# Two chunks per key-value step in alternating row halves, and the bf16 copy of the state moved to VectorE

## The chip, the cores and the metric

The kernel runs on all 8 cores of one Trainium2 chip. Each core computes one sequence of the batch of 8 on its own; there is no exchange between cores. The metric is the device time in microseconds of the slowest core. TensorE (PE in the profile) multiplies, ScalarE (ACT) applies functions, VectorE (DVE) does elementwise arithmetic, GpSimd (POOL) and SyncE (SP) only start transfers here.

## What is computed

Two layers over x of 8 x 4096 x 1024. The part that the change touches is the gated linear attention: per head (4 heads, keys of 128, values of 256) a state of 128 x 256 is carried from one chunk of 64 frames to the next, and every frame of a chunk reads the state at the end of its own chunk.

```python
proj = jnp.einsum('bsd,de->bse', h, w_in[l])
q, k, v, r, fz, gb_in, gc_in, cx, ga, gb = jnp.split(proj, split_pts, axis=-1)
...
kd = kc * jnp.exp(cum_end - cum)                  # decay of each key to chunk end (<= 1)
gamma = jnp.exp(cum_end[:, :, :, 0, :])           # whole-chunk decay (n_chunks,B,H,HEAD_K)
def step(state, inp):
    q_i, kd_i, v_i, g_i = inp
    state = g_i[..., None] * state + jnp.einsum('bhlk,bhlv->bhkv', kd_i, v_i)
    o_i = jnp.einsum('bhlk,bhkv->bhlv', q_i, state)
    return state, o_i
...
o = o * lax.rsqrt(jnp.mean(o * o, axis=-1, keepdims=True) + NORM_EPS) * gla_norm_g[l]
o = o.reshape(b_sz, s_len, VAL_WIDTH).astype(x.dtype) * jax.nn.silu(r)
y_a = jnp.einsum('bsv,vd->bsd', o, w_oa[l])
conv = causal_depthwise_conv(gc_in * cx, conv_w[l], conv_b[l])
y_b = jnp.einsum('bsc,cd->bsd', gb_in * conv, w_ob[l])
mix = jax.nn.sigmoid(ga) * y_a + jax.nn.sigmoid(gb) * y_b
x = x + jnp.einsum('bsd,de->bse', mix, w_o[l])
hid = jax.nn.silu(h2 @ w_ffn_gate[l]) * (h2 @ w_ffn_up[l])   # h2 = RMSNorm(x)
x = x + jnp.einsum('bsf,fd->bsd', hid, w_ffn_down[l])
```

## The kernel before, in words

A core works on tiles of 512 frames: 8 tiles per layer, 16 in all. A tile's token mixing (`mix_units`) and the feed-forward part of the tile before it (`ffn_units`) are lists of units with a cost; `woven` merges the two lists by these costs, and every engine gets its instructions in the order in which the units are then called. So the order on each engine is fixed when the program is built. Tile 0 has no feed-forward work beside it, the 15 tiles after it have.

A usual unit is a group of 8 matmuls of 128 x 512 (L278) into one of four PSUM banks, `banks`, which are handed round as a ring; the engine that reads the bank last gives it back. TensorE can thus run at most four units ahead of the engines that empty the banks. The units that matter here:

- `u_r` (8 per tile): the output gate r. ScalarE computes the sigmoid in three steps, L300, L302, L304, and VectorE multiplies (L307, output in `dgm`) and frees the bank. `u_g` of the feed-forward part is of the same kind (output in `sg`), `u_u` needs only VectorE (L307, output in `hid`).
- `u_C`, `u_X`, `u_B` (8 each per tile): the convolution branch, with L519 on ScalarE and L307, L537, L540, L542 on VectorE.
- `g_U` (8 calls per tile, 128 in all): the key-value products. A slice `ts` of 128 frames holds two chunks, c = 0 in partitions 0 to 63 and c = 1 in partitions 64 to 127. Each call issues four matmuls with 64 rows, then VectorE updates four states (L454) and ScalarE copies each to bf16 (L458).
- `g_C` (4 calls per tile): eight matmuls of queries with the bf16 states (L472), then on ScalarE four squares with sums (L482), L486 and L488, then L492 on VectorE. `g_T`: transposes (L504), copied by VectorE (L511).

In the list, `g_U` stands behind unit ts*8 and behind unit ts*8+2 of the r and convolution units, `g_C` behind ts*8+5, `g_T` behind ts*8+9. The eight r units come first, so the two calls of `g_U` and the `g_C` of slice 0 lie among them.

`Eng.after` sets a wait only if the engine hasn't yet waited for that value. The banks of `g_U` are `BU = (4, 5)`, which the norms use too (`BN1`, `BN2`). S32 are four states in fp32, S16 are eight bf16 copies, one for each chunk and head.

Of the kernel before, what the change touches and what calls it, by code (L numbers as in the profile page):

```python
# [8 lines left out]
AF = mybir.ActivationFunctionType  # L9
ALU = mybir.AluOpType  # L10
# [79 lines left out]
def build_nc(S):  # L90
# [12 lines left out]
    with ExitStack() as es:  # L103
        newsem = lambda n: es.enter_context(nc.semaphore(n))
        sb = lambda n, s, d: es.enter_context(nc.sbuf_tensor("sb_" + n, s, d))
        pe = Eng(nc.tensor, newsem("s_pe"))
        act = Eng(nc.scalar, newsem("s_act"))
        dve = Eng(nc.vector, newsem("s_dve"))
        pool = Eng(nc.gpsimd, newsem("s_pool"))
        sp = Eng(nc.sync, newsem("s_sp"))  # L110
        V, A, P = nc.vector, nc.scalar, nc.tensor
# [6 lines left out]
        kd = sb("kd", [128, NTS, 512], BF16)  # L118
# [214 lines left out]
        def mix_units(i):  # L333
# [2 lines left out]
            us = []  # L336
            loc = {"spb": [None] * 4, "dec": [None] * 4, "v": [None] * 8, "kd": [None] * 4, "q": [None] * 4,
                   "grs": [[None, None] for _ in range(4)], "og": [None] * 4, "ogT": [None] * 4, "gbc": [None] * 8,
                   "mix": [None] * 8, "sg": {}, "S16": {}, "x": [None] * 8, "sp_used": None, "nmm": None, "n2mm": None}

            def add(cost, blk, fn):
                us.append(Unit(cost, (i, BIDX[blk]) if blk else None, fn))
# [92 lines left out]
                sg.give(buf, loc["grs"][ts][hf])  # L435


            def g_U(ts, c):
                pr = slice(c * 64, (c + 1) * 64)
                for hp in range(2):  # L440
                    pe.after(loc["kd"][ts], loc["v"][hp * 4 + ts], st["U_free"][hp])
                    for h2_ in range(2):
                        hh = hp * 2 + h2_
                        ins = P.matmul(pb[BU[hp]][:, h2_ * 256:(h2_ + 1) * 256], kd[pr, ts, hh * 128:(hh + 1) * 128],  # L444
                                       vog[pr, ts, hh * 256:(hh + 1) * 256], start=True, stop=True)
                    k = pe.do(ins)
# [408 lines left out]
```

How the kernel before makes its waits and increments, by code:

```python
    def after(self, *toks):  # L57
        for tk in toks:
            if tk is None:
                continue
            sem, val = tk
            if self.seen.get(id(sem), 0) < val:
                self.h.wait_ge(sem, val)
                self.seen[id(sem)] = val
# [1 line left out]
    def do(self, ins):  # L66
        ins.then_inc(self.sem, 1)
        self.n += 1
        return (self.sem, self.n)
# [20 lines left out]
def build_nc(S):  # L90
# [74 lines left out]
        def load(q, dst, src, name):
            s = newsem(name)
            q.h.dma_start(out=dst, in_=src).then_inc(s, 16)
            return (s, 16)
        t_id = load(act, ident32[:], cst_d[:, 0:128], "c_id")
        t_msk = load(act, msk[:], cst_d[:, 128:258], "c_msk")
        t_pk = load(act, pk[:], pk_d, "c_pk")
        wfg_sem = newsem("c_wfg")
        nc.scalar.dma_start(out=wfg[0:17, :], in_=wfg_d[0]).then_inc(wfg_sem, 16)
        t_wfg = (wfg_sem, 16)
        t_ones = dve.do(V.memset(ones16[:], 1.0 / D))
        t_eps = dve.do(V.memset(epsb[:], EPS))
# [20 lines left out]
        def load_x(i):  # L199
            l, t = divmod(i, NT)
            b = i % 3
            if xs_n[b]:
                sp.after((xstore[b], xs_n[b]))
            if l == 0:
                src = x_d[:, t * T:(t + 1) * T].rearrange("(c p) s -> p c s", p=128)
            else:
                sp.after(spill[t])
                src = xs_d[t].rearrange("p (c s) -> p c s", c=KC)
            nc.sync.dma_start(out=xT[b][:], in_=src).then_inc(xland[b], 16)
            xl_n[b] += 16
            st["x", i] = (xland[b], xl_n[b])
```

## Time and profile before

| | |
|---|---|
| median of 3 runs | 5062.94 us |
| profiled execution, time | 5063.73 us |
| its span (core 7, the slowest) | 5062.7 us |
| spans of the 8 cores | 5041.4 to 5062.7 us |
| mean granted TensorE clock, core 7 | 0.975 |
| busy share: PE, ACT, DVE, POOL | 95%, 44%, 41%, 4% |

TensorE is busy almost all the time; the other engines matter where it waits for them. The views used are the waits of each engine (who waited for whom, and how long), the timeline (instructions in order of time, those of a kind merged), the groups of instructions, and the windows (busy time of each engine in a stretch).

### The profile page before, as it was taken

To read this page: it belongs to the slowest core of one execution; us is meant where nothing else is said; L and a number is where in the kernel's file an instruction comes from. 1 tells how busy PE (TensorE), PEld (TensorE's weight loads), DVE (VectorE), ACT (ScalarE), POOL (GpSimd) and SP (SyncE) were. 2 spreads that over 40 slices of the span, in tenths; PEclk is the share of its full clock that TensorE was granted. 3 is DMA by queue.
4 is the path that set the end of the run, shared out by engine and by line. 5 is a ranking of instruction groups with operands and counts; after the bars stand their busy time and mean duration, and the time that the engine had idled before them with its cause. 6 is when DMAs were issued, how large, how long until landed. Compare 5 with 4: busy or idle time off the path is not lost.

```text
span 5062.7 us, 66511 instructions; the slowest of 8 cores (5041.4 to 5062.7 us)
## 1 busy us (share of the span) xinstructions
PE 4811.1 (95%) x22464; PEld 2165.7 (43%) x22464; DVE 2086.6 (41%) x3486; ACT 2218.1 (44%) x4481; POOL 189.8 (4%) x362
## 2 busy tenths in 40 slices
PE   6999999999999999999899999999999999999998
PEld 2444444444444444444344444434444444444443
DVE  2544353433535345253252534435344353443633
ACT  3454353544535444353343544435344354543533
POOL 0000000000000000000000000000000000000000
PEclk9999999999999999999899999999999999999999
DMA  6768989786553444444567888877755444343343
GB/s 136 136 130 153 193 158 207 180 201 185 168 183 127 138 158 142 154 140 139 126 134 172 146 163 176 174 190 181 190 192 165 159 140 148 140 150 137 134 153 116
DMA packets 131197, 798.91 MB, mean 158 GB/s; under 512 B 13074, under 2 KB 13330, under 8 KB 66612
## 3 DMA queue, kind: packets, MB, share of 16 engines
q0 software_dynamic: 51552, 336.81, 34.3%
q1 hardware_dynamic: 78866, 457.64, 26.2%
q8 instruction: 189, 3.10, 0.2%
q14 instruction: 140, 1.15, 0.1%
q10 hardware_dynamic: 450, 0.22, 0.0%
HBM read 936.24 MB, written 114.36 MB: 208 GB/s over the span
## 4 chain that ended last, share of the span: by engine, by line
PE 81%; ACT 6%; DMA 4%; DVE 4%; issue 3%; ACTq 0%; DVEq 0%; POOL 0%; SPq 0%; POOLq 0%
PE pb L278 75%; ACT sb_sg L302 2%; ACT sb_sg L300 2%; DMA scr<-sb_wsl 2%; DVE sb_h L329 1%; PE pb L404 1%; DMA sb_wsl<-w 1%; PE pb L317 1%; PE pb L444 1%; PE pb L393 1%; ACT sb_sg L304 1%; DVE sb_xT L329 1%; DMA sb_xT<-x 1%; PE pb L380 1%; ACT sb_sqj L482 1%
## 5 line engine op out<-in xcount | busy, mean ns | idle before, releaser
L278 PE MATMUL pb<-sb_h,sb_wsl 128*128 128x512 bf16 (+1 forms) x11392 | 2630.3, 384 | 86.5 <-DVE sb_dgm L307 32.5
L278 PEld LDWEIGHTS pb<-sb_h,sb_wsl 128*128 128x128 bf16 (+1 forms) x11392 | 1103.8, 99 | 1478.7 <-issue 242.7
L307 DVE TENSOR_TENSOR sb_sg<-pb,sb_sg 128x512 f32<-128x512 f32 x608 | 418.2, 691 | 1485.2 <-ACT sb_sg L304 1012.3
L300 ACT ACTIVATE sb_sg<-pb 128x512 f32<-128x512 f32 x736 | 434.4, 590 | 1178.5 <-PE pb L278 1178.3
L278 PE MATMUL pb<-sb_hid,sb_wsl 128*128 128x512 bf16 x2816 | 631.4, 380 | 9.7 <-DMA sb_wsl<-w 7.5
L278 PE MATMUL pb<-sb_wsl,sb_h 128*128 128x512 bf16 x2560 | 621.2, 392 | 5.3 <-DVE sb_sg L307 3.5
L302 ACT ACTIVATE sb_sg<-sb_sg 128x512 f32<-128x512 f32 x736 | 464.1, 631 | 69.8 <-ACT sb_sg L300 3.0
L304 ACT ACTIVATE sb_sg<-sb_sg 128x512 f32<-128x512 f32 x736 | 464.0, 630 | 68.8 <-ACT sb_sg L302 1.8
L278 PEld LDWEIGHTS pb<-sb_hid,sb_wsl 128*128 128x128 bf16 x2816 | 275.4, 98 | 344.3 <-issue 19.1
L278 PEld LDWEIGHTS pb<-sb_wsl,sb_h 128*128 128x128 bf16 x2560 | 253.5, 101 | 355.4 <-issue 93.3
L313 ACT ACTIVATE sb_sq<-sb_xT 128x512 bf16<-128x512 f32 x320 | 195.9, 623 | 403.7 <-DVE sb_xT L604 322.3
L307 DVE TENSOR_TENSOR sb_hid<-pb,sb_sg 128x512 bf16<-128x512 f32 x352 | 241.7, 687 | 212.6 <-PE pb L278 206.5
L715 DVE TENSOR_TENSOR sb_xT<-pb,sb_xT 128x512 f32<-128x512 f32 x128 | 88.4, 691 | 584.2 <-PE pb L278 584.2
L458 ACT ACTIVATE sb_S<-sb_S 128x256 bf16<-128x256 f32 x512 | 203.2, 417 | 261.5 <-DVE sb_S L454 260.2
L278 PE MATMUL pb<-sb_vog,sb_wsl 128*128 128x512 bf16 x1024 | 255.4, 395 | 33.5 <-DVE sb_vog L511 33.5
L238 POOL DMA_DIRECT2D sb_wsl<-w x272 | 143.9, 530 | 3671.4 <-PE pb L278 2853.8
L278 PE MATMUL pb<-sb_dgm,sb_wsl 128*128 128x512 bf16 x1024 | 241.7, 379 | 16.3 <-DVE sb_dgm L583 16.3
L278 PE MATMUL pb<-sb_sgc,sb_wsl 128*128 128x512 bf16 x1024 | 243.0, 380 | 0.0
L454 DVE SCALAR_TENSOR_TENSOR sb_S<-sb_S,sb_gam,pb 128x256 f32<-128x256 f32 x512 | 210.7, 473 | 0.0
L329 DVE SCALAR_TENSOR_TENSOR sb_h<-sb_xT,sb_pk,sb_rstd 128x512 bf16<-128x512 f32 x256 | 180.6, 744 | 59.7 <-ACT sb_rstd L326 59.7
L317 PE MATMUL pb<-sb_sq,sb_ones 128*128 128x512 bf16 x320 | 115.7, 384 | 60.2 <-ACT sb_sq L313 60.2
L278 PEld LDWEIGHTS pb<-sb_vog,sb_wsl 128*128 128x128 bf16 x1024 | 101.6, 100 | 162.3 <-issue 50.5
(58 smaller groups left out, 2404.5 us busy)
## 6 DMA issues: line engine op xcount, KB each, us to landing
sb_wsl<-scr SPq DMA_DIRECT2D x248, 1024.0 KB, 5.1
sb_wsl<-w POOLq DMA_DIRECT2D x168, 1024.0 KB, 10.4
sb_wsl<-scr SPq DMA_DIRECT2D x76, 768.0 KB, 4.9
sb_wsl<-scr SPq DMA_DIRECT2D x80, 704.0 KB, 4.2
scr<-sb_wsl POOLq DMA_DIRECT2D x52, 1024.0 KB, 13.6
sb_wsl<-w POOLq DMA_DIRECT2D x52, 768.0 KB, 8.4
sb_wsl<-w POOLq DMA_DIRECT2D x48, 704.0 KB, 8.7
sb_xT<-x SPq DMA_DIRECT2D x8, 2048.0 KB, 20.8
```

The source lines that it names most:

```text
L238: nc.gpsimd.dma_start(out=wsl[s][:, 0:n], in_=blk_ap(w_d, l, bi)).then_inc(wsem_p[s], 16)
L278: ins = P.matmul(out, a, b, start=(j == 0), stop=(j == n - 1))
L300: k = act.do(A.activation(out=buf[:], in_=pb[b][:, :], func=AF.Exp, scale=-1.0))
L302: k = act.do(A.activation(out=buf[:], in_=buf[:], func=AF.Ln, bias=1.0))
L304: return buf, act.do(A.activation(out=buf[:], in_=buf[:], func=AF.Exp, scale=-1.0))
L307: return V.tensor_tensor(out=out, in0=a, in1=b, op=ALU.mult)
L313: k = act.do(A.activation(out=buf[:], in_=xT[xb][:, dc, :], func=AF.Square))
L317: kk = pe.do(P.matmul(pb[bank][:, :], ones16[:, :], buf[:], start=(dc == 0), stop=(dc == KC - 1)))
L329: return V.scalar_tensor_tensor(out=out, in0=xT[xb][:, dc, :], scalar=pkc(gcol), in1=rs[:], op0=ALU.mult, op1=ALU.mult)
L454: ks = dve.do(V.scalar_tensor_tensor(out=S32[hh][:], in0=S32[hh][:], scalar=gam[:, g:g + 1], in1=pb[BU[hp]][:, h2_ * 256:(h2_ + 1) * 256], ...
L458: loc["S16"][hh] = act.do(A.activation(out=S16[si][:], in_=S32[hh][:], func=AF.Copy))
L715: k = dve.do(V.tensor_tensor(out=xT[xb][:, dc, :], in0=pb[b][:, :], in1=xT[xb][:, dc, :], op=ALU.add))
```

## The change: what it does

A call of `g_U` no longer takes one chunk and four heads, but two heads and both chunks. Its four matmuls alternate between rows 0 to 63 and rows 64 to 127, and chunk c writes bank `BU[c]` where before head pair hp wrote `BU[hp]`. One wait for both banks stands ahead of all four. VectorE then updates the two states for chunk 0, copies them to bf16 itself, updates them for chunk 1 and copies them. ScalarE's 512 copies are gone. Numbers and sizes of all other instructions stay.

```diff
-            def g_U(ts, c):
-                pr = slice(c * 64, (c + 1) * 64)
-                for hp in range(2):
-                    pe.after(loc["kd"][ts], loc["v"][hp * 4 + ts], st["U_free"][hp])
-                    for h2_ in range(2):
-                        hh = hp * 2 + h2_
-                        ins = P.matmul(pb[BU[hp]][:, h2_ * 256:(h2_ + 1) * 256], kd[pr, ts, hh * 128:(hh + 1) * 128],
+            def g_U(ts, hp):
+                pe.after(loc["kd"][ts], loc["v"][hp * 4 + ts], st["U_free"][0], st["U_free"][1])
+                for h2_ in range(2):
+                    hh = hp * 2 + h2_
+                    for c in range(2):
+                        pr = slice(c * 64, (c + 1) * 64)
+                        ins = P.matmul(pb[BU[c]][:, h2_ * 256:(h2_ + 1) * 256], kd[pr, ts, hh * 128:(hh + 1) * 128],
                                        vog[pr, ts, hh * 256:(hh + 1) * 256], start=True, stop=True)
...
+                for c in range(2):
                     for h2_ in range(2):
                         hh = hp * 2 + h2_
                         g = ts * 8 + hh * 2 + c
-                        si = (c * 4 + hh)
-                        dve.after(k, loc["gam"], st["S32"][hh], loc["S16"].get(hh))
+                        dve.after(k, loc["gam"], st["S32"][hh])
                         ks = dve.do(V.scalar_tensor_tensor(out=S32[hh][:], in0=S32[hh][:], scalar=gam[:, g:g + 1],
-                                                           in1=pb[BU[hp]][:, h2_ * 256:(h2_ + 1) * 256], op0=ALU.mult, op1=ALU.add))
+                                                           in1=pb[BU[c]][:, h2_ * 256:(h2_ + 1) * 256], op0=ALU.mult, op1=ALU.add))
                         st["S32"][hh] = ks
-                        act.after(ks, st["S16_used"][si])
-                        loc["S16"][hh] = act.do(A.activation(out=S16[si][:], in_=S32[hh][:], func=AF.Copy))
-                        loc["S16", c, hh] = loc["S16"][hh]
-                        st["gam_used"] = ks
-                    st["U_free"][hp] = ks
+                    st["U_free"][c] = ks
+                    for h2_ in range(2):
+                        hh = hp * 2 + h2_
+                        si = c * 4 + hh
+                        dve.after(st["S32"][hh], st["S16_used"][si])
+                        loc["S16", c, hh] = dve.do(V.tensor_copy(out=S16[si][:], in_=S32[hh][:]))
+                st["gam_used"] = ks
```

On TensorE, the second call of slice 0 in the sixth tile (kd holds the keys, vog the values, pb4 and pb5 are the two banks), before:

```order
L278 MATMUL pb3<-sb_h2,sb_wsl0 128x512 x7
L444 MATMUL pb4<-sb_vog,sb_kd 128x256 [waits s_dve]
L444 MATMUL pb4<-sb_vog,sb_kd 128x256
L444 MATMUL pb5<-sb_vog,sb_kd 128x256 [waits s_dve]
L444 MATMUL pb5<-sb_vog,sb_kd 128x256
L278 MATMUL pb0<-sb_wsl3,sb_h1 128x512 [waits s_dve]
```

The same place now:

```order
L278 MATMUL pb3<-sb_h2,sb_wsl0 128x512 x7
L445 MATMUL pb4<-sb_vog,sb_kd 128x256 [waits s_dve]
L445 MATMUL pb5<-sb_vog,sb_kd 128x256
L445 MATMUL pb4<-sb_vog,sb_kd 128x256
L445 MATMUL pb5<-sb_vog,sb_kd 128x256
L278 MATMUL pb0<-sb_wsl3,sb_h1 128x512 [waits s_dve]
```

Still four key-value matmuls between the same two units, but neighbours now use different row halves and different banks, and the second wait has moved to the front.

On VectorE, the same call, before (sb_S32 are the states, sb_dgm the output of an r unit):

```order
L307 TENSOR_TENSOR sb_sg0<-pb3,sb_sg0 128x512 [waits s_act]
L454 SCALAR_TENSOR_TENSOR sb_S32_0<-sb_S32_0,sb_gam,pb4 128x256 [waits s_pe,s_dve]
L454 SCALAR_TENSOR_TENSOR sb_S32_1<-sb_S32_1,sb_gam,pb4 128x256 [waits s_dve]
L454 SCALAR_TENSOR_TENSOR sb_S32_2<-sb_S32_2,sb_gam,pb5 128x256 [waits s_pe,s_dve]
L454 SCALAR_TENSOR_TENSOR sb_S32_3<-sb_S32_3,sb_gam,pb5 128x256 [waits s_dve]
L307 TENSOR_TENSOR sb_dgm<-pb0,sb_sg1 128x512 [waits s_act]
```

And now:

```order
L307 TENSOR_TENSOR sb_sg0<-pb3,sb_sg0 128x512 [waits s_act]
L455 SCALAR_TENSOR_TENSOR sb_S32_2<-sb_S32_2,sb_gam,pb4 128x256 [waits s_pe]
L455 SCALAR_TENSOR_TENSOR sb_S32_3<-sb_S32_3,sb_gam,pb4 128x256
L463 CAST sb_S16_2<-sb_S32_2 128x256 [waits s_dve]
L463 CAST sb_S16_3<-sb_S32_3 128x256 [waits s_dve]
L455 SCALAR_TENSOR_TENSOR sb_S32_2<-sb_S32_2,sb_gam,pb5 128x256
L455 SCALAR_TENSOR_TENSOR sb_S32_3<-sb_S32_3,sb_gam,pb5 128x256
L463 CAST sb_S16_6<-sb_S32_2 128x256 [waits s_dve]
L463 CAST sb_S16_7<-sb_S32_3 128x256 [waits s_dve]
L307 TENSOR_TENSOR sb_dgm<-pb0,sb_sg1 128x512 [waits s_act]
```

Between the same two neighbours VectorE has eight instructions where it had four.

On ScalarE, the same call, before:

```order
L304 ACTIVATE sb_sg0<-sb_sg0 128x512 [waits s_act]
L458 ACTIVATE sb_S16_4<-sb_S32_0 128x256 [waits s_dve]
L458 ACTIVATE sb_S16_5<-sb_S32_1 128x256 [waits s_dve]
L458 ACTIVATE sb_S16_6<-sb_S32_2 128x256 [waits s_dve]
L458 ACTIVATE sb_S16_7<-sb_S32_3 128x256 [waits s_dve]
L300 ACTIVATE sb_sg1<-pb0 128x512 [waits s_pe]
```

And now:

```order
L302 ACTIVATE sb_sg0<-sb_sg0 128x512 [waits s_act]
L304 ACTIVATE sb_sg0<-sb_sg0 128x512 [waits s_act]
L300 ACTIVATE sb_sg1<-pb0 128x512 [waits s_pe,s_dve]
L302 ACTIVATE sb_sg1<-sb_sg1 128x512 [waits s_act]
L304 ACTIVATE sb_sg1<-sb_sg1 128x512 [waits s_act]
```

The next sigmoid (L300 on bank 0) follows the one before it directly; the four copies, with their waits for VectorE, no longer stand between.

## Rows read from the trace of the kernel before

**Rows 1.** The page's first line.

```profile
span 5062.7 us, 66511 instructions; the slowest of 8 cores (5041.4 to 5062.7 us)
```

**Rows 2.** TensorE's waits: us in total, times, longest us.

```profile
PE pb L278 <- DVE sb_dgm L307: 34.0, 28, 1.9
...
PE pb L278 <- DMA sb_wsl<-w: 14.1, 4, 5.8
...
PE pb L278 <- DVE sb_hid L307: 7.5, 8, 2.2
```

**Rows 3.** Groups by line: busy us, mean ns | idle before, releaser.

```profile
L444 PE MATMUL pb<-sb_vog,sb_kd 64*128 64x256 bf16 x512 | 78.3, 272 | 3.7 <-DVE sb_S L454 3.7
...
L458 ACT ACTIVATE sb_S<-sb_S 128x256 bf16<-128x256 f32 x512 | 203.2, 417 | 261.5 <-DVE sb_S L454 260.2 <-issue 1.3
```

**Rows 4.** Timeline, one call of g_U: start us, us, engine, line.

```profile
1300.79 0.38 PE L278 MATMUL pb<-sb_h,sb_wsl 128*128 128x512 bf16 x1
1301.10 0.61 PE L444 MATMUL pb<-sb_vog,sb_kd 64*128 64x256 bf16 x4
...
1301.64 0.39 PE L278 MATMUL pb<-sb_h,sb_wsl 128*128 128x512 bf16 x1
```

**Rows 5.** Timeline, one call of g_C.

```profile
1316.34 0.38 PE L278 MATMUL pb<-sb_h,sb_wsl 128*128 128x512 bf16 x1
...
1316.65 0.63 PE L472 MATMUL pb<-sb_S,sb_qT 128*64 128x256 bf16 x8
...
1317.21 0.39 PE L278 MATMUL pb<-sb_h,sb_wsl 128*128 128x512 bf16 x1
```

**Rows 6.** Timeline of the sixth tile, around the second call for slice 0.

```profile
1561.12 1.89 PE L278 MATMUL pb<-sb_wsl,sb_h 128*128 128x512 bf16 x8
...
1564.08 0.69 DVE L307 TENSOR_TENSOR sb_sg<-pb,sb_sg 128x512 f32<-128x512 f32 x1 [1.24 <-ACT sb_sg L304]
...
1564.57 3.62 PE L278 MATMUL pb<-sb_wsl,sb_h 128*128 128x512 bf16 x16
1564.68 1.64 DVE L454 SCALAR_TENSOR_TENSOR sb_S<-sb_S,sb_gam,pb 128x256 f32<-128x256 f32 x4
1565.25 1.59 ACT L458 ACTIVATE sb_S<-sb_S 128x256 bf16<-128x256 f32 x4 [1.27 <-DVE sb_S L454]
1566.74 0.58 ACT L300 ACTIVATE sb_sg<-pb 128x512 f32<-128x512 f32 x1
...
1569.15 0.69 DVE L307 TENSOR_TENSOR sb_dgm<-pb,sb_sg 128x512 bf16<-128x512 f32 x1 [2.82 <-ACT sb_sg L304]
...
1569.99 1.89 PE L278 MATMUL pb<-sb_h,sb_wsl 128*128 128x512 bf16 x8 [1.80 <-DVE sb_dgm L307]
```

**Rows 7.** The same tile, 10 us later, behind g_C of slice 0.

```profile
1577.49 0.58 ACT L300 ACTIVATE sb_sg<-pb 128x512 f32<-128x512 f32 x1
1577.56 1.89 PE L278 MATMUL pb<-sb_h,sb_wsl 128*128 128x512 bf16 x8
...
1580.46 1.89 PE L278 MATMUL pb<-sb_h,sb_wsl 128*128 128x512 bf16 x8 [1.01 <-DVE sb_dgm L307]
```

**Rows 8.** VectorE groups, SBUF to SBUF with one tensor operand.

```profile
L537 DVE TENSOR_SCALAR sb_csb<-sb_ub,sb_pk 128x512 f32<-128x512 f32 x128 | 69.9, 546 | 14.2 <-DVE sb_ub L307 0.5
...
L181 DVE CAST sb_ident<-sb_ident 128x128 bf16<-128x128 f32 x1 | 0.2, 227 | 1.4 <-DMA sb_ident<-cst 1.4
```

**Rows 9.** Timeline of the sixth tile, second call for slice 2.

```profile
1617.39 8.81 PE L278 MATMUL pb<-sb_h,sb_wsl 128*128 128x512 bf16 x40
...
1621.01 1.65 DVE L454 SCALAR_TENSOR_TENSOR sb_S<-sb_S,sb_gam,pb 128x256 f32<-128x256 f32 x4
1622.58 0.68 DVE L307 TENSOR_TENSOR sb_sgc<-pb,sb_csb 128x512 bf16<-128x512 f32 x1
```

**Rows 10.** Window in tile 0: PE, PEld, DVE, ACT, POOL busy us (xcount), clock, DMA.

```profile
115.00:175.00 60.00, 53.04 (x283) 23.81 (x281) 47.40 (x91) 31.29 (x99) 4.22 (x8) 1.00 0.74 130
```

**Rows 11.** GpSimd's weight loads, from the page's groups.

```profile
L238 POOL DMA_DIRECT2D sb_wsl<-w x272 | 143.9, 530 | 3671.4 <-PE pb L278 2853.8
```

More of the change, by code:

```diff
@@ L338, in mix_units @@
                    "grs": [[None, None] for _ in range(4)], "og": [None] * 4, "ogT": [None] * 4, "gbc": [None] * 8,
-                   "mix": [None] * 8, "sg": {}, "S16": {}, "x": [None] * 8, "sp_used": None, "nmm": None, "n2mm": None}
+                   "mix": [None] * 8, "sg": {}, "x": [None] * 8, "sp_used": None, "nmm": None, "n2mm": None}
             def add(cost, blk, fn):
@@ L435, in u_r @@
                 sg.give(buf, loc["grs"][ts][hf])
-            def g_U(ts, c):
-                pr = slice(c * 64, (c + 1) * 64)
-                for hp in range(2):
-                    pe.after(loc["kd"][ts], loc["v"][hp * 4 + ts], st["U_free"][hp])
-                    for h2_ in range(2):
-                        hh = hp * 2 + h2_
-                        ins = P.matmul(pb[BU[hp]][:, h2_ * 256:(h2_ + 1) * 256], kd[pr, ts, hh * 128:(hh + 1) * 128],
+            def g_U(ts, hp):
[5 more added lines that the diff above has]
+                        ins = P.matmul(pb[BU[c]][:, h2_ * 256:(h2_ + 1) * 256], kd[pr, ts, hh * 128:(hh + 1) * 128],
                                        vog[pr, ts, hh * 256:(hh + 1) * 256], start=True, stop=True)
-                    k = pe.do(ins)
-                    loc["U", ts] = k
-                    st["kd_used"] = k
+                k = pe.do(ins)
+                loc["U", ts] = k
+                st["kd_used"] = k
+                for c in range(2):
                     for h2_ in range(2):
```

## The prediction

> **What bounds the kernel now.** I read the page first: TensorE is busy 95% of a span of 5062.7 us [rows 1], ScalarE 44% and VectorE 41%. So a faster ScalarE or VectorE is worth nothing by itself. Two things count: time that TensorE's own work takes, and the places where TensorE waits. For these the view is TensorE's waits [rows 2]: the largest entry that the other engines' attention work can touch is that for `dgm`, the output of the r units, 34.0 us in 28 waits; beside it stand 7.5 us for `hid`, which VectorE issues right behind it, and 14.1 us for weight loads, which the edit does not touch. Then comes the timeline around such a wait in an ordinary tile [rows 6, 7], since a wait for VectorE need not be VectorE's fault. The profiled execution took 5063.73 us, 0.8 us over the median of 5062.94, so a sum made against the trace holds for the median too.
>
> **Part 1, the four products in alternating row halves.** Before, a call's four matmuls of 256 columns use the same 64 rows. They start 0.113 us apart, (0.61 - 0.27) / 3 [rows 3, 4], so each streams alone. From the last ordinary matmul ahead (1300.79) to the first behind (1301.64) pass 0.85 us; less one ordinary pitch of 0.22 us (1.73 us for a unit of eight, which is 8.81 less the last one's 0.38, over 39 [rows 9]) the call costs 0.63 us. The trace does not show row halves side by side, so I bound the gain. One end is nothing: the halves take turns, and the call stays at 0.63. The other is the nearest row, `g_C` [rows 5], which uses half the array in columns: its eight matmuls of the same 256 columns cost 1317.21 - 1316.34 - 0.22 = 0.65 us, as much as four of `g_U`. So there two share the time of one. If alternating rows do the same, two pitches of 0.113 go from each call, less some nanoseconds: 0.20 us. Over 128 calls that is 25.5 us, all of it on TensorE, which is the bound. I take this end, since `g_C` is the same engine with the same column count and the new order puts independent halves and separate banks next to each other. A loss is excluded by the count: no matmul, weight load or switch between full and half array is added, each call had one of either before.
>
> **Part 2, ScalarE loses 512 copies** (203.2 us of busy time, and another 261.5 us in which it stood in front of them waiting, nearly all of it for L454 [rows 3]). Most of this ran beside other work. Where it does not is seen in rows 6. TensorE runs the r unit of bank 0 from 1561.12, done by 1563.01. ScalarE would be free for its sigmoid right behind the sigmoid that VectorE reads at 1564.08, that is at about 1564.0, but next in its queue are the four copies, and these wait for the updates, which VectorE starts only at 1564.68. So the sigmoid starts at 1566.74, 2.7 us late; VectorE multiplies at 1569.15, and TensorE, four banks ahead, waits for bank 0 and resumes at 1569.99. Its last matmul had started at 1564.57 + 3.62 - 0.38 = 1567.81, so it could have gone on at 1568.03: 1.96 us lost, of which the profile calls 1.80 a wait.
>
> With the copies gone from ScalarE the product is ready for VectorE at about 1569.15 - 2.74 = 1566.4. Now VectorE is next late: its group is longer by four casts. Their duration is not in the trace at this size. The nearest rows are the cast of 128 elements, 227 ns, and the one-tensor operation of 512, 546 ns [rows 8]; between them 256 elements come to 333 ns. Ends: 227 ns, and 546 ns. Queued instructions overlap by 0.08 us (L454 takes 0.47 and has a pitch of (1.64 - 0.47) / 3 = 0.39), so I take a pitch of 0.25 us, 1.0 us for four. The group before took 1622.58 - 1621.01 = 1.57 us to the next instruction [rows 9]. Then L307 starts at 1564.68 + 1.57 + 1.0 = 1567.25, TensorE 0.84 us later (as 1569.15 to 1569.99) at 1568.09, against 1568.03 if nothing held it. The stall is gone but for 0.06 us. I count 1.8 us for each of the 15 tiles that have feed-forward work beside them: 27 us. That the sixth tile is typical follows from the sums: (34.0 + 7.5) / 15 = 2.8 us of waits per tile [rows 2], and it has 1.80 + 1.01 [rows 6, 7].
>
> The second stall of the tile [rows 7] stands behind `g_C`, whose squares and sums keep ScalarE's queue. TensorE's last matmul there started at 1577.56 + 1.89 - 0.38 = 1579.07, and it resumes at 1580.46: 1.17 us lost. ScalarE is 2.74 us earlier at the first place and TensorE 1.96, so at most 0.8 of the 1.17 can go, and nothing need go if ScalarE then waits for its own inputs. I take 0.5: 15 x 0.5 = 7.5 us. Together part 2 gives 34.5 us.
>
> **Part 3, what the longer group on VectorE costs.** Queued behind it are the multiplications that free TensorE's banks. The tightest place that I found outside the r units is in rows 9: L307 ends at 1623.26 and frees the bank that the unit starting at 1617.39 + 4 x 1.73 = 1624.31 needs, 1.05 us to spare, of which 0.15 is the release itself (1569.99 less 1569.84). So 0.9 us covers an addition of 1.0: 0.1 x 15 = 1.5 us lost. In tile 0, without feed-forward units between, VectorE is busy 47.4 of 60 us [rows 10] and TensorE waits for it already; six calls fall there, 6 x 1.0 = 6 us if all is exposed, nothing if ScalarE's relief covers it. I take 4. The wait for both banks at the front of a call costs nothing in the other tiles: the updates that free bank 5 end at 1622.66, and the next call is behind the 40 matmuls. `g_C` now waits for VectorE's casts in place of ScalarE's copies: it stood 3 units behind them and keeps that. If this cover fails each cast costs its 0.25 us.
>
> **Sum:** 5063.7 - 25.5 - 34.5 + 1.5 + 4 = 5009.2, so 5009 us, 1.1% below.
>
> **Rivals.**
>
> 1. The halves take turns (or the products are done one by one for another reason; the change then does not do what it says on TensorE). For it: no row shows row halves overlapping, and in `g_C` neighbours in the order are of the same column half, so what overlaps there is not fully clear. Time: 5009 + 25.5 = 5035.
> 2. The ScalarE stall is replaced by one of VectorE of the same size: VectorE is behind for a reason of its own, and the wait at `dgm` keeps its length. For it: after the change VectorE is the one that is late at rows 6, by my own sum only 0.06 us from the point. Against: the earlier copies also held ScalarE back, so the whole stretch should run earlier. Time: 5009 + 34.5 = 5044.
> 3. Slower: casts that do not overlap, since each follows an update that it depends on. With 546 ns each and 0.1 us between, the group grows by a = 2.6 us. The first stall keeps a - 0.94 = 1.66 of its 1.96 us (gain 0.3 x 15 = 4.5), the place in rows 9 loses a - 0.9 = 1.7 x 15 = 25.5, tile 0 loses 6 x 2.6 = 15.6: 5063.7 - 25.5 - 4.5 + 25.5 + 15.6 = 5075. It decides from a of about 2.3 us (gains 25.5 + 9, losses 21 + 13.8). Against it: the 227 ns of the cast in rows 8.
> 4. More is gained: both stalls go whole (1.96 + 1.17 = 3.1 us, 15 x 3.0 = 45) and tile 0 costs nothing: 5063.7 - 25.5 - 45 = 4993.
> 5. The casts delay GpSimd's weight loads. There are 272 [rows 11]; TensorE waits for them 14.1 us in four waits [rows 2]. If a load lands later by a call's four casts, 4 x 0.33 = 1.3 us, and a quarter of them have no time to spare, 68 x 1.3 = 88 us: 5097. It turns the result from (5063.7 - 5009) / 1.3 = 42 such loads. The Trainium skill states such a rule (SBUF — State Buffer, Who interferes with whom): a VectorE copy or cast from SBUF to SBUF may take the port pair that it shares with GpSimd, and GpSimd, which writes the descriptors of its own DMAs, is then shut out for the whole instruction. The trace speaks neither for nor against: VectorE's one-tensor operations of 546 ns [rows 8] are already there beside these loads, and the loads' only long waits are for TensorE to free a slot [rows 11], which suggests time to spare.
>
> **How the numbers follow.** The forecast, 5009 with some 10 us either way for the terms that I split, has 0.55; rival 4 has 0.12, rival 1 0.12, rival 2 0.10, rival 3 0.06, rival 5 0.02, and 0.03 is left for what I have not seen. The range goes from 4988 (rival 4 and 5 us for a TensorE clock that changes level at other moments) to 5044 (rival 2, which with rival 1 it takes in); rivals 3 and 5 are left out. A measurement of this kernel can tell a change from none at about 2%, 101 us. All stalls and the products together are worth 71 us, so faster by more than that has 0.01; slower by more needs rival 5 at twice its price, 0.01; within it 0.98.
>
> **What would show it.** A call on TensorE of 0.43 us, its four starts in two pairs; if they stay 0.11 apart, part 1 is wrong. No wait for `dgm` of over 1 us in the r stretch; if one stays, the timeline must tell whether VectorE's casts or a sigmoid came last. Casts of 0.33 us with a pitch of 0.25. VectorE busy some 128 to 170 us more, ScalarE 203 us less. In tile 0 some microseconds more of waits for the updates. I would be wrong altogether if VectorE's group ran past 3.9 us, or if waits for weight loads grew beyond their 14.1 us.

## The result, and the profile after

The changed kernel took 4998.45, 5006.16 and 5009.74 us, the kernel before 5062.35 and 5062.94 in the same comparison; the ratio is 0.9886, with a 95% interval of 0.9857 to 0.9914. That is 1.1% or 57.7 us less: clear of no change by its interval, but under the 2% that the prediction named as the bound. One execution of the change (5521.09) and two of before (5207.78, 5729.62) had a die at a lower clock and are left out, which is why the medians over all executions, 5007.95 against 5135.36, lie 2.5% apart. The profiled execution after is that of 4998.45 us.

The page of the kernel after, its first lines:

```profile
span 4997.4 us, 65713 instructions; the slowest of 8 cores (4979.2 to 4997.4 us)
...
PE 4736.9 (95%) x22021; PEld 2137.6 (43%) x22464; DVE 2185.6 (44%) x3998; ACT 2025.8 (41%) x3969; POOL 190.5 (4%) x362
```

The same line of the page before:

```profile
PE 4811.1 (95%) x22464; PEld 2165.7 (43%) x22464; DVE 2086.6 (41%) x3486; ACT 2218.1 (44%) x4481; POOL 189.8 (4%) x362
```

The span fell from 5062.7 us [rows 1] by 65.3 us. VectorE was busy 2086.6 us before and 2185.6 now, ScalarE 2218.1 and 2025.8. TensorE's busy sum has 443 matmul records fewer than the 22464 weight loads, so it can't be set against that of before; starts and waits can.

TensorE's waits after (us in total, times, longest us):

```profile
PE pb L278 <- DVE sb_vog L514: 33.3, 15, 3.8
...
PE pb L278 <- DMA sb_wsl<-w: 15.2, 5, 4.8
...
PE pb L445 <- DVE sb_S L455: 6.7, 4, 2.1
PE pb L278 <- DVE sb_dgm L307: 5.8, 8, 1.0
PE pb L278 <- DVE sb_hid L307: 4.6, 8, 2.2
PE pb L475 <- DVE sb_S L463: 1.1, 2, 0.7
```

Against [rows 2] the wait for `dgm` went from 34.0 to 5.8 us and that for `hid` from 7.5 to 4.6, together 31.1 us. Waits for weight loads stand at 15.2 against 14.1. Waits for the states grew: the products' for the updates from 3.7 us [rows 3] to 6.7, and `g_C` now waits 1.1 us for the casts. All of these stand in tile 0.

The groups of after that answer to [rows 3] and [rows 11]:

```profile
L445 PE MATMUL pb<-sb_vog,sb_kd 64*128 64x256 bf16 x512 | 50.2, 274 | 6.7 <-DVE sb_S L455 6.7
...
L463 DVE CAST sb_S<-sb_S 128x256 bf16<-128x256 f32 x512 | 125.1, 284 | 1.4 <-DVE sb_S L463 1.3
...
L238 POOL DMA_DIRECT2D sb_wsl<-w x272 | 144.3, 531 | 3612.5 <-PE pb L278 2687.5
```

One matmul of the products lasts as long as before, 274 against 272 ns, but the 512 together cover 50.2 us of the clock on the wall against 78.3: they overlap. The new casts take 284 ns, and VectorE stood idle only 1.4 us ahead of all of them.

The timeline of one call of `g_U` after, against [rows 4]:

```profile
1538.26 0.38 PE L278 MATMUL pb<-sb_wsl,sb_h 128*128 128x512 bf16 x1
1538.57 0.39 PE L445 MATMUL pb<-sb_vog,sb_kd 64*128 64x256 bf16 x4
1538.89 0.39 PE L278 MATMUL pb<-sb_wsl,sb_h 128*128 128x512 bf16 x1
```

Four products now last 0.39 us where they lasted 0.61. In the records of single matmuls the starts stand at 0, 3, 119 and 123 ns, in two pairs, where before they stood at 0, 120, 229 and 338. From the last ordinary matmul to the next ordinary one pass 0.636 us, the median of the calls, against 0.852.

The timeline of after at the place of [rows 6], the second call for slice 0 in the sixth tile:

```profile
1548.28 0.60 ACT L300 ACTIVATE sb_sg<-pb 128x512 f32<-128x512 f32 x1
1548.47 0.69 DVE L307 TENSOR_TENSOR sb_sg<-pb,sb_sg 128x512 f32<-128x512 f32 x1 [1.24 <-ACT sb_sg L304]
...
1549.08 0.86 DVE L455 SCALAR_TENSOR_TENSOR sb_S<-sb_S,sb_gam,pb 128x256 f32<-128x256 f32 x2
...
1549.69 3.62 PE L278 MATMUL pb<-sb_wsl,sb_h 128*128 128x512 bf16 x16
...
1549.86 0.49 DVE L463 CAST sb_S<-sb_S 128x256 bf16<-128x256 f32 x2
1550.26 0.86 DVE L455 SCALAR_TENSOR_TENSOR sb_S<-sb_S,sb_gam,pb 128x256 f32<-128x256 f32 x2
1551.04 0.48 DVE L463 CAST sb_S<-sb_S 128x256 bf16<-128x256 f32 x2
1551.45 0.68 DVE L307 TENSOR_TENSOR sb_dgm<-pb,sb_sg 128x512 bf16<-128x512 f32 x1
...
1553.14 1.89 PE L278 MATMUL pb<-sb_h,sb_wsl 128*128 128x512 bf16 x8
```

The sigmoid of bank 0 starts at 1548.28, ahead of the updates, where before it stood behind the copies. VectorE multiplies for `dgm` right behind its last cast, and is done at 1552.13; TensorE's last matmul starts at 1549.69 + 3.62 - 0.38 = 1552.93 and the next r unit follows it at 1553.14 with no wait, 1.0 us after the product was ready. And at the place of [rows 7], behind `g_C`:

```profile
1560.60 0.60 ACT L300 ACTIVATE sb_sg<-pb 128x512 f32<-128x512 f32 x1 [0.22 <-issue]
1560.72 1.89 PE L278 MATMUL pb<-sb_h,sb_wsl 128*128 128x512 bf16 x8
...
1562.74 0.69 DVE L307 TENSOR_TENSOR sb_dgm<-pb,sb_sg 128x512 bf16<-128x512 f32 x1 [0.53 <-ACT sb_sg L304]
...
1563.58 1.89 PE L278 MATMUL pb<-sb_h,sb_wsl 128*128 128x512 bf16 x8 [0.97 <-DVE sb_dgm L307]
```

This one is still there, 0.97 us against 1.01, for ScalarE still comes out of `g_C`'s squares late. On this core the sixth tile lost more at it (1.13 us) than the other tiles of the layer (0.85). All the waits for `dgm` that are left are of this kind.

**The account.** Products: 128 calls x (0.852 - 0.636) = 27.6 us. Waits for `dgm` and `hid`: 31.1 us. Another way to count the second gives nearly the same on every core: in the stretch of the r units of the 15 tiles, the sum of what TensorE's starts came late beyond their pitch of 0.217 us fell from 43.1 to 10.6 us. Together 58.7 us. Against it, the waits for the states in tile 0 grew by 4.1 us, while the transposes' wait there for `ogtok`, 1.5 us before, is gone:

```profile
PE pb L504 <- DVE sb_ogtok L492: 1.5, 1, 1.5
```

That leaves 56.1 us, beside the 57.7 of the ratio. The mean of the eight spans, 5051.9 before, is 4987.9, 4991.6 and 4994.1 in the three executions after: 57.8 to 64.0 us less. So the account closes within the spread of the executions.

### The profile page after: what moved, and what is told of

Its sections match the earlier page's. It is cut to its first block, busy times and chain, and to the rows that moved or that the text cites. A ratio compares the mean times of both kernels' runs of the same rounds, so it can differ in the third digit from the quotient of the medians.

```text
span 4997.4 us, 65713 instructions; the slowest of 8 cores (4979.2 to 4997.4 us)
## 1 busy us (share of the span) xinstructions
PE 4736.9 (95%) x22021; PEld 2137.6 (43%) x22464; DVE 2185.6 (44%) x3998; ACT 2025.8 (41%) x3969; POOL 190.5 (4%) x362
## 3 DMA queue, kind: packets, MB, share of 16 engines
q1 hardware_dynamic: 78866, 457.64, 26.2%
## 4 chain that ended last, share of the span: by engine, by line
PE 82%; DMA 7%; DVE 5%; ACT 4%; issue 3%; POOL 0%; DVEq 0%; ACTq 0%; POOLq 0%; SPq 0%
PE pb L278 76%; DMA scr<-sb_wsl 3%; DMA sb_wsl<-w 2%; DVE sb_h L329 1%; PE pb L404 1%; PE pb L317 1%; PE pb L393 1%; ACT sb_sg L302 1%; ACT sb_sg L300 1%; DVE sb_xT L329 1%; DMA sb_xT<-x 1%; ACT sb_sg L304 1%; PE pb L445 1%; PE pb L475 1%; DVE sb_sg L307 1%
## 5 line engine op out<-in xcount | busy, mean ns | idle before, releaser
L278 PE MATMUL pb<-sb_h,sb_wsl 128*128 128x512 bf16 (+1 forms) x11139 | 2608.4, 384 | 80.5 <-DVE sb_fza L365 26.7
L278 PEld LDWEIGHTS pb<-sb_h,sb_wsl 128*128 128x128 bf16 (+1 forms) x11392 | 1103.0, 99 | 1451.1 <-issue 211.3
L307 DVE TENSOR_TENSOR sb_sg<-pb,sb_sg 128x512 f32<-128x512 f32 x608 | 418.0, 691 | 1403.0 <-ACT sb_sg L304 935.7
L300 ACT ACTIVATE sb_sg<-pb 128x512 f32<-128x512 f32 x736 | 435.4, 592 | 1286.7 <-PE pb L278 1229.9
L278 PE MATMUL pb<-sb_hid,sb_wsl 128*128 128x512 bf16 x2774 | 631.2, 381 | 13.4 <-DMA sb_wsl<-w 7.9
L278 PE MATMUL pb<-sb_wsl,sb_h 128*128 128x512 bf16 x2494 | 604.5, 387 | 10.8 <-DVE sb_sg L307 4.5
L278 PEld LDWEIGHTS pb<-sb_hid,sb_wsl 128*128 128x128 bf16 x2816 | 276.2, 98 | 346.9 <-issue 22.8
L278 PEld LDWEIGHTS pb<-sb_wsl,sb_h 128*128 128x128 bf16 x2560 | 251.6, 100 | 346.9 <-issue 80.7
L307 DVE TENSOR_TENSOR sb_hid<-pb,sb_sg 128x512 bf16<-128x512 f32 x352 | 241.7, 687 | 204.6 <-PE pb L278 198.5
L278 PE MATMUL pb<-sb_vog,sb_wsl 128*128 128x512 bf16 x1024 | 255.4, 395 | 33.4 <-DVE sb_vog L514 33.3
L278 PE MATMUL pb<-sb_dgm,sb_wsl 128*128 128x512 bf16 x987 | 239.6, 379 | 18.2 <-DVE sb_dgm L586 16.3
L278 PE MATMUL pb<-sb_sgc,sb_wsl 128*128 128x512 bf16 x979 | 235.1, 379 | 2.4
L455 DVE SCALAR_TENSOR_TENSOR sb_S<-sb_S,sb_gam,pb 128x256 f32<-128x256 f32 x512 | 221.1, 473 | 0.0
L536 ACT ACTIVATE sb_halo<-sb_ub 128x2 f32<-128x2 f32 x128 | 26.0, 204 | 359.6 <-DVE sb_ub L307 359.6
L278 PEld LDWEIGHTS pb<-sb_vog,sb_wsl 128*128 128x128 bf16 x1024 | 101.8, 100 | 163.2 <-issue 52.3
## 6 DMA issues: line engine op xcount, KB each, us to landing
sb_wsl<-w POOLq DMA_DIRECT2D x168, 1024.0 KB, 10.9
```

The lines of the kernel that those rows point to most:

```text
L278: ins = P.matmul(out, a, b, start=(j == 0), stop=(j == n - 1))
L300: k = act.do(A.activation(out=buf[:], in_=pb[b][:, :], func=AF.Exp, scale=-1.0))
L307: return V.tensor_tensor(out=out, in0=a, in1=b, op=ALU.mult)
```

## The experiments

In each diff + and - are against the changed kernel, except for the second, whose is against the kernel before. Below, "late starts" is the sum just told: 43.1 us before, 10.6 us after.

**One: the pairs alone, copies on ScalarE.** This undoes part 2. The updates write one state per head, so each must wait for the copy of the one before.

```diff
-                        dve.after(k, loc["gam"], st["S32"][hh])
+                        dve.after(k, loc["gam"], st["S32"][hh], st.get(("cp", hh)))
...
-                        dve.after(st["S32"][hh], st["S16_used"][si])
-                        loc["S16", c, hh] = dve.do(V.tensor_copy(out=S16[si][:], in_=S32[hh][:]))
+                        act.after(st["S32"][hh], st["S16_used"][si])
+                        loc["S16", c, hh] = act.do(A.activation(out=S16[si][:], in_=S32[hh][:], func=AF.Copy))
+                        st["cp", hh] = loc["S16", c, hh]
```

> Part 1 alone: the four products alternate between the row halves as in the change, but ScalarE makes the bf16 copies. Since chunk 1 overwrites the same fp32 state in the same call, VectorE must now wait in the middle of its group for ScalarE's copies of chunk 0. Theory (the two parts are independent gains, the products are worth 27.6 us = 128 x 0.216 us): about 5035 us against 5063 before, and the wait for dgm stays at some 34 us. Rival (the two parts need each other: the middle wait holds up both queues): waits for dgm grow to 50 us or more and the time comes out at 5045 to 5065, most of the products' gain given back.

It took 5056.79 and 5064.24 us, against 5058.12 to 5064.35 for the kernel before on the same chip (and once 5092.06): nothing gained that the slowest core shows; no interval is on record for it. Yet the call takes 0.636 us as in the change. TensorE's waits of this kernel:

```profile
PE pb L278 <- DVE sb_dgm L307: 49.4, 31, 3.3
...
PE pb L278 <- DVE sb_hid L307: 5.3, 5, 2.2
```

The timeline of it at the second call for slice 0 of a tile:

```profile
1571.76 0.86 DVE L455 SCALAR_TENSOR_TENSOR sb_S<-sb_S,sb_gam,pb 128x256 f32<-128x256 f32 x2
...
1572.32 0.81 ACT L463 ACTIVATE sb_S<-sb_S 128x256 bf16<-128x256 f32 x2 [1.27 <-DVE sb_S L455]
...
1572.84 0.87 DVE L455 SCALAR_TENSOR_TENSOR sb_S<-sb_S,sb_gam,pb 128x256 f32<-128x256 f32 x2 [0.22 <-ACT sb_S L463]
...
1573.42 0.81 ACT L463 ACTIVATE sb_S<-sb_S 128x256 bf16<-128x256 f32 x2 [0.29 <-DVE sb_S L455]
1574.13 0.58 ACT L300 ACTIVATE sb_sg<-pb 128x512 f32<-128x512 f32 x1
```

Now both engines wait for each other in the middle of the group: chunk 1's updates for chunk 0's copies (0.22), then ScalarE for these updates (0.29). The sigmoid starts 2.37 us after the first update, where in [rows 6] it was 1566.74 - 1564.68 = 2.06. Late starts grew to 57 to 61 us on the eight cores, some 16 us more than before, which takes back more than half of the 27.6. They are not waits alone: behind the longest of them TensorE's matmuls start 0.43 us apart for a while and not 0.22, at a granted clock of 0.55 in such a stretch (core 7, 963 to 966 us), and 2 to 6 us of each core's sum are of this kind. The mean of the eight spans is 5042.1 and 5048.1 us, against 5047.1 to 5055.2 before on that chip (5058.6 in the long one), so some 6 us are left of the gain. The rival held, with 49.4 us of waits where it said 50 or more: the products in pairs need the copies moved. With one state per head, the order that pairs them also ties the copies between the updates.

**Two: the casts alone, products in the old order.**

```diff
-                        dve.after(k, loc["gam"], st["S32"][hh], loc["S16"].get(hh))
+                        dve.after(k, loc["gam"], st["S32"][hh])
...
-                        act.after(ks, st["S16_used"][si])
-                        loc["S16"][hh] = act.do(A.activation(out=S16[si][:], in_=S32[hh][:], func=AF.Copy))
...
+                    for h2_ in range(2):
+                        hh = hp * 2 + h2_
+                        si = c * 4 + hh
+                        dve.after(st["S32"][hh], st["S16_used"][si])
+                        loc["S16", c, hh] = dve.do(V.tensor_copy(out=S16[si][:], in_=S32[hh][:]))
```

> Part 2 alone: a call takes one chunk and four heads as before, its products one after another in one row half, but VectorE makes the bf16 copies. Theory: a call on TensorE still costs 0.63 us, the first stall of a tile (1.96 us) goes, the second shrinks by 0.3 to 0.7 us: 5063 - 15 x 2.3 = 5029 us, waits for dgm under 8 us. Rival (the stalls went because the shorter calls gave VectorE and ScalarE time): waits for dgm stay near 34 us and the time near 5063.

Measured: ratio 0.9938 (0.9905 to 0.9971), 5023.89, 5029.92, 5033.28 and 5052.54 us; the profiled execution is the last. Its waits:

```profile
PE pb L278 <- DVE sb_dgm L307: 5.8, 8, 1.0
PE pb L278 <- DVE sb_hid L307: 4.6, 8, 2.2
```

They are those of the change to the tenth, late starts are 10.6 us, and the call still takes 0.852 us. So part 2 alone removes the stalls, and does nothing else.

**Three: another order within the call.** First both heads of chunk 0, then both of chunk 1, so that neighbours in the order use the same 64 rows.

```diff
-                for h2_ in range(2):
-                    hh = hp * 2 + h2_
-                    for c in range(2):
+                for c in range(2):
+                    for h2_ in range(2):
+                        hh = hp * 2 + h2_
```

> The change with its four products in another order: both heads of chunk 0 (rows 0 to 63), then both of chunk 1. Same banks, same waits, same work elsewhere. Theory (two products share time only if they are neighbours in different row halves): only the second and third overlap, a call costs 0.11 us more than in the change, 128 x 0.11 = 14 us: about 5022 us, starts at 0, 0.12, 0.12 and 0.23 us. Rival (any two products of a call in half-array tiles overlap, as the neighbours of the same column half seem to do in g_C): the same as the change, 5008 us.

Measured: ratio 0.988 (0.9842 to 0.9918), 5003.62 to 5012.05 us. The timeline of a call:

```profile
1564.90 0.38 PE L278 MATMUL pb<-sb_h,sb_wsl 128*128 128x512 bf16 x1
1565.21 0.40 PE L445 MATMUL pb<-sb_vog,sb_kd 64*128 64x256 bf16 x4
1565.54 0.39 PE L278 MATMUL pb<-sb_h,sb_wsl 128*128 128x512 bf16 x1
```

The call takes 0.640 us, the same as with neighbours in alternate halves, and the records show the starts at 0, 7, 119 and 126 ns. My theory that each must find its partner right beside it would have lost half of the gain, and it fell. What counts is that both row halves have work within the call. The records don't name the half of a product, so which two start together is not shown. The doubt in rival 1 has the same answer: in `g_C` [rows 5], where two products of one column half stand before two of the other, the eight starts come in pairs too, 7 ns apart.

**Four: longer casts.** Each of the casts issued twice, the second waiting for the first.

```diff
-                        loc["S16", c, hh] = dve.do(V.tensor_copy(out=S16[si][:], in_=S32[hh][:]))
+                        for _ in range(2):
+                            loc["S16", c, hh] = dve.do(V.tensor_copy(out=S16[si][:], in_=S32[hh][:]))
+                            dve.after(loc["S16", c, hh])
```

> The change with every bf16 cast on VectorE issued twice, each waiting for the one before: a call's group on VectorE grows by four casts, some 1.6 us at 0.28 us and 0.1 us between, from 2.37 to about 4.0 us. It measures the cover of VectorE. Theory (VectorE's queue has about 1.0 us to spare at the first stall and 0.3 us at the place of the second call of slice 2): 0.6 us comes back per tile at the first and 1.3 us at the other, and tile 0 loses 6 x 1.6 us: 15 x 1.9 + 10 = 38 us, about 5046 us. Rival (VectorE is idle over half of the time and covers it): within 8 us of the change.

None of its times (5452.9 us and up) can be set against the others. But single cores can: the 18 whose granted clock was 0.967 or more took 5101.5 to 5157.7 us, 5136 in the mean, where such cores of the kernel before took 5060 on that chip. With the 57.7 us that the change gains, this is some 130 us above the change, over three times what I had expected. Part of it is that the dose was larger: VectorE's group took 4.80 us in the median, not 4.0, since casts that wait for each other start 0.40 us apart. The waits of its core 7:

```profile
PE pb L278 <- DVE sb_sgc L307: 54.2, 39, 2.8
PE pb L278 <- DVE sb_hid L307: 24.4, 31, 2.2
PE pb L278 <- DVE sb_dgm L307: 18.0, 31, 1.1
```

The largest new wait is not in the r stretch but behind slice 2 (`sgc`), the place of [rows 9]. For a price from whole executions I tried a smaller dose.

**Five: two casts more per call.** Chunk 1's two are issued again.

```diff
+                    for h2_ in range(2 * c):
+                        hh = hp * 2 + h2_
+                        si = c * 4 + hh
+                        dve.after(loc["S16", c, hh])
+                        loc["S16", c, hh] = dve.do(V.tensor_copy(out=S16[si][:], in_=S32[hh][:]))
```

> The changed kernel with the two casts of chunk 1 issued a second time: a call's group on VectorE grows by two casts, some 0.5 to 0.6 us. It measures VectorE's cover with half the dose of the run with every cast doubled. Theory (the tightest place outside the r units has 0.1 to 0.3 us to spare, the first stall 1.0 us): 0.4 us lost per tile outside the r stretch, 0.2 in it, 3 us in tile 0: about 12 us over the change, ratio 0.991. Rival (cover is exceeded at several places of a tile at once): 25 us or more, ratio above 0.993, with waits for sgc and hid that the change does not have.

Measured: ratio 0.9913 (0.9896 to 0.993), where the change itself, run beside it, has 0.9888; 0.25%, 12.7 us, about what I had expected, though the intervals overlap. The group grew by 0.40 us (2.78 against 2.37). But the loss is not where I had put it. Of its waits:

```profile
PE pb L278 <- DVE sb_dgm L307: 5.8, 8, 1.0
...
PE pb L278 <- DVE sb_sgc L307: 3.2, 8, 0.7
```

The wait for `dgm` did not move, and late starts in the r stretch are 10.9 us; a stretch later, at `sgc`, TensorE is late by 4 to 5.4 us in all, where the change has 0 to 1.3. So the tight place is that of [rows 9], and the r stretch has cover. The other 8 us are in no wait, and most of them are in the clock: 384 ordinary matmuls of a core, in the mean, start 0.43 us after the one before them and not 0.22, against 337 in the change beside it. At 0.21 us each that is 9.8 us, though such counts differ by 18 between two executions of the change (319 and 337).

**Six: copies on ScalarE again, but with a state of their own for chunk 0,** so that chunk 1's updates need not wait for a copy. Eight states in place of four, the first plan, don't fit: 416 bytes of a partition's SBUF are left where the squares' scrap output needs 512, so that version has no result. This one has six, and to make room, the scrap output of the squares shares memory with the 32-bit identity matrix, which has been read by then.

```diff
-        S32 = [sb("S32_%d" % h, [128, 256], F32) for h in range(4)]
+        S32 = [sb("S32_%d" % h, [128, 256], F32) for h in range(6)]
...
-                        ks = dve.do(V.scalar_tensor_tensor(out=S32[hh][:], in0=S32[hh][:], scalar=gam[:, g:g + 1],
+                        ks = dve.do(V.scalar_tensor_tensor(out=(S32[hh] if c else S32[4 + h2_])[:], in0=(S32[4 + h2_] if c else S32[hh])[:], scalar=gam[:, g:g + 1],
```

> Products in pairs, copies on ScalarE, and two more fp32 states in place of four: chunk 0 of a call writes a state of its own, from which ScalarE copies and chunk 1 updates, so VectorE waits in a call for no copy of that call. (The scrap output of L482 shares memory with a constant that is no longer read.) Against the first run (one set of states, 49.4 us of waits for dgm) it gives the price of the middle wait. Theory (that wait is what costs): waits for dgm back to about 34 us, time 5035 us or ratio 0.994. Rival (ScalarE's copies cost as much wherever VectorE waits, because they come in two halves of a call now): waits stay near 49 us, ratio 0.999.

Measured: ratio 0.9962 (0.9946 to 0.9977), 5048.77 to 5053.47 us. Its waits:

```profile
PE pb L278 <- DVE sb_dgm L307: 41.9, 33, 2.3
...
PE pb L278 <- DVE sb_hid L307: 7.4, 8, 2.2
```

Late starts are 50.5 us. So the wait in the middle of the group, seen in experiment one, costs about 8 us (57 to 61 less 50.5, the lower clock behind it included), and copies that come in two halves on ScalarE cost some 7 us beyond those of before (50.5 less 43.1). My theory had only the first: waits for `dgm` are 41.9 us, halfway between its 34 and the rival's 49. The sum closes: 27.6 - 7.4 = 20.2 us, and 0.38% of 5063 is 19.2.

**Seven and eight: the largest wait that is left.** The biggest entry that this part of the kernel has after the change is `L278 <- DVE sb_vog`, 33.3 us: the gate units that follow `u_v` wait for VectorE's copies of `vog`. The edit puts the transposes of slice 3, `g_T(3)`, ahead of the first two gate units.

```diff
-                add(8, n, lambda dc=dc: u_gate(dc, 0))
-                add(8, n, lambda dc=dc: u_gate(dc, 1))
                 if dc == 0:
                     add(3, None, lambda: g_T(3))
+                add(8, n, lambda dc=dc: u_gate(dc, 0))
+                add(8, n, lambda dc=dc: u_gate(dc, 1))
```

> The change with the last g_T of a tile put ahead of the first two gate units in place of behind them. It is a trial for a faster version: in the changed kernel TensorE waits 33.3 us in 15 waits for VectorE's copy of that transpose, and runs 8 matmuls at the lower clock behind each such wait of 3.7 us. Theory: with two units between the transpose and its first reader the wait goes whole, and the clock stays up: 15 x (2.2 + 1.7) = 58 us, about 4950 us. Rival (VectorE's copy is queued behind a product that waits for ScalarE, and stays late): 10 to 25 us, 4985 to 4998 us.

> The early transpose again, beside the change on one chip. Theory: the change's 33.3 us of waits for vog are gone, about 2.2 us in each of 15 tiles, but only part of the clock that follows them comes back: 30 to 45 us below the change, ratio to before 0.980 to 0.983. Rival (the first result came from a chip that differs): under 20 us below the change.

Measured: ratios 0.9822 (0.9781 to 0.9863), 4982.86 to 5030.52 us, and, on another chip, 0.9806 (0.9787 to 0.9824), 4965.72 to 4974.88 us. The waits and the cores of the second run:

```profile
PE pb L278 <- DVE sb_vog L514: 0.5, 1, 0.5
```

```profile
core 1: 4964.7 us, clock 0.979
```

The wait is gone, 33.3 to 0.5 us. On this chip it is 0.8% below the change, some 41 us, as the second expectation had it; the 58 us of the first fell. 33 of the 41 are the wait, and the clock gives the rest. The timeline of the change at one of these waits, and the window of the eight matmuls behind it:

```profile
1653.37 3.19 PE L278 MATMUL pb<-sb_vog,sb_wsl 128*128 128x512 bf16 x8 [3.73 <-DVE sb_vog L514]
```

```profile
1653.40:1656.30 2.90, 2.90 (x8) 1.07 (x9) 0.00 (x0) 0.00 (x0) 0.00 (x0) 0.57 0.02 6
```

At a granted clock of 0.57, near the lower of TensorE's two levels (1.2 of 2.4 GHz), eight matmuls last 3.19 us where they otherwise take 1.89. Only 9 of the 15 waits are longer than 1 us, and behind nearly all of these, 5 to 10 matmuls start so far apart; the first expectation had counted 8 behind each of the 15. Over a core, starts 0.43 us apart fell from 337 to 297 in the mean, and 40 x 0.21 = 8.4 us. It is the fastest version here, though its gain has nothing to do with the change under study.

**Nine: the change once more, on the chip of experiments five, six and eight.**

> The changed kernel as it is, on the chip on which the next three run, so that they can be compared with it directly and not only by way of the kernel before. Every theory expects the ratio measured first, 0.986 to 0.991.

Measured: ratio 0.9888 (0.9859 to 0.9917), with 5.8 us in 8 waits for `dgm` again.

## Why the prediction was right in its time, and the step that failed

**Time.** Forecast 5009 us from a range of 4988 to 5044, measured 5007.95 in the median; -1.1% forecast, -1.1% measured. The sum counted 54.5 us of gain (25.5 + 34.5 - 1.5 - 4), the ratio gives 57.7, and the mean of the spans 57.8 to 64.0. The mechanism, products in pairs and ScalarE's queue, held. That the sum came so near is in part luck, for its terms missed in both directions.

**The step that failed is part 3, the price of the longer group on VectorE:** 5.5 us were counted, and 1.7 to 3.0 came. In tile 0, TensorE's waits for the states grew by 4.1 us, which is the 4 of the prediction. But they are not what the tile lost, since 0.9 us of waits for `dgm` and 1.5 us for `ogtok` went in the same tile; 1.7 us net. With the 1.7 us that its eight calls gain by the pairs, the way from its first product to the next tile's first takes 214.3 to 217.4 us on the eight cores, where before it took 216.1 to 218.4. The prediction had named ScalarE's relief as the possible cover and given it too little. The place in [rows 9] loses 0 to 1.3 us on a core, as told (1.5). With this the sum closes: 27.6 for the products, 26.2 and 5.5 for the two stalls by TensorE's starts, less 1.7 and 0 to 1.3, is 56.3 to 57.6 us. The window of [rows 10] after, in the same columns:

```profile
115.00:175.00 60.00, 52.93 (x275) 23.53 (x279) 49.05 (x109) 19.25 (x69) 4.87 (x9) 0.97 0.70 125
```

The tile's work stands 3 to 4 us later in this window than before, so it only shows the direction: ScalarE fell from 31.29 to about 19 us, VectorE rose by 2, and TensorE's busy time stayed.

**Part 1, the products: 25.5 us forecast, 27.6 measured.** The bound that I took, `g_C`'s column halves as the measure for row halves, held to 2 us: 0.216 us of a call against 0.20. It was the riskiest step, resting on a row of another shape, and experiment three shows that its reason was only half understood: I leaned on the new order's putting independent halves next to each other, and the order makes no difference.

**Part 2, the stalls: 34.5 us forecast, 31.1 to 32.5 measured.** That ScalarE's queue, and not VectorE's work, made the stall is shown by experiment two, which moves only the casts and has all of it gone. By starts, the first stall of the 15 tiles cost 26.2 us and is gone whole (27 forecast). Its margin was wrong all the same: -0.06 us forecast, while the product was ready at 1552.13, could have let TensorE go on at 1552.29 (0.84 behind L307's start, as in the prediction), and TensorE went on at 1553.14, 0.85 us later. Two terms make the difference. The group grew by a = 2.37 - 1.57 = 0.80 us (1551.45 - 1549.08, against [rows 9]), not 1.0: the cast takes 284 ns, not 333, and has a pitch of 0.49 - 0.28 = 0.21, not 0.25. And VectorE came to the place 0.73 us earlier: it began the multiplication ahead of the group 1.22 us before TensorE began its 16 matmuls (1548.47, 1549.69), where before it was 0.49 us (1564.08, 1564.57 [rows 6]). The sum had kept VectorE's start fixed. Rival 2 had named the reason against itself, that the earlier copies held ScalarE back too; that this is why VectorE came earlier was not tested by itself. The second stall gave less: 16.1 us in the 15 tiles before and 10.6 after, so 5.5 us or 0.37 per tile, not 0.5. In layer 0 1.17 us became 0.85 to 1.1, in layer 1 0.87 became 0.51. Here ScalarE's own squares and sums rule, as the prediction feared.

**The rivals.** Rival 1 (halves take turns) is refuted by the pairs of starts. Rival 2 (VectorE takes the stall's place) by the 0.85 us to spare. Rival 3 turns on a of 2.3 us; a is 0.80. Experiments four and five show that the mechanism is real though: VectorE's group has cover for its present length and little more, and what gives way first is the place of [rows 9], not that of [rows 6], as the prediction had it. With a = 3.2 (4.80 - 1.57) experiment four did come out slower than the kernel before. Rival 4 (4993) needed the second stall gone and tile 0 free; 10.6 us of the one stayed and the other cost 1.7.

Rival 5, a delay of GpSimd's weight loads: with 512 casts more the issue of a load takes 531 ns against 530, and the median from issue to landing is 10.9 us against 10.4. TensorE's waits for loads are 15.2 us against 14.1, so by the letter the prediction's sign of being wrong altogether, waits grown beyond 14.1, has come. But it was no usable sign. Within one execution these waits run from 3.0 to 18.3 us over the eight cores before and from 7.3 to 17.3 after. Experiment one, which has no casts on VectorE, has 19.0 us and a landing of 11.2 on its slowest core; experiment two, which has all of them, 8.9 and 10.5. So an effect of 88 us is ruled out, and one of a few us could not be seen. No run here shows the rule that the prediction took from the Trainium skill (SBUF — State Buffer, Who interferes with whom) at work.

**The signatures.** A call of 0.43 us with its starts in pairs (0.636 - 0.217 = 0.42), no wait for `dgm` over 1 us (longest 1.0), ScalarE 203 us less (192) held. VectorE was to be busy 128 to 170 us more and was 99 more. The step there added up durations: the casts are 125.1 us by themselves, but each pair of casts overlaps the updates beside it by some 0.08 us at each end (1549.08 + 0.86 = 1549.94, where the first casts start at 1549.86), so updates and casts together cover 314.8 us where the updates covered 210.7, 104 more. The rest of VectorE's work is unchanged: 1892.9 us before and 1890.8 after, taken by itself.

**What stays open** is which two products of a call run side by side, and what makes the second stall shrink by just 0.37 us.

## What to carry to other kernels

When a wait names VectorE, look one engine further back: here VectorE was in time, and it was ScalarE's queue that held, with a copy at its head that waited for VectorE while a ready sigmoid stood behind it; moving the 417 ns copy onto the engine that makes its input made it a 284 ns cast and removed 31 us of TensorE's waits. Products that fill half of the array are worth giving to TensorE in one go, both halves in the same call, but then also look at which buffers the new order ties together, for here the pairs alone gained nothing that the slowest core shows. When costing the moved work, take the whole stretch as it will run, with the earlier removals in it, and don't keep the start times of the profile before.

## What the runs showed of the hardware

- Half-array matmuls of 256 columns overlap when the two row halves are both in the call, whatever their order in it: four cost 0.42 us beyond the ordinary pitch both with neighbours in alternate halves (0.636 us between ordinary starts) and with neighbours in the same half (0.640), and 0.63 when all are in one half (0.852). How far apart in the order the partners may stand was not tried.
- Two pairs at the pitch of 0.12 us explain 0.24 of these 0.42 us. The rest, about 0.2 us for each call, lies at its two edges: from the last ordinary start to the first product and from the last product to the next ordinary start pass 0.51 us together, before and after (0.852 - 0.338, 0.636 - 0.123). That the change between whole and half array makes it was not tested.
- A cast of 128x256 from fp32 to bf16 takes 284 ns on VectorE with 0.2 us between starts, the copy of the same tile on ScalarE 417 ns with 0.39.
- After a wait of 3.73 us TensorE ran eight matmuls of 512 columns in 3.19 us, at a granted clock of 0.57, where eight otherwise take 1.89. So a stall can cost more than its wait: removing 33 us of such waits gave some 41.
